# Scaling the long filter by its energy through four columns of short-convolution weights instead of through its spectrum

## What is computed

```python
def long_conv_bidir(u, h, bias):
    L = u.shape[1]
    k = jnp.concatenate([h[:, 0], jnp.zeros((1, HY_WIDTH), f32), h[:0:-1, 1]], axis=0)
    k = k * lax.rsqrt(jnp.sum(k * k, axis=0, keepdims=True))
    kf = jnp.fft.rfft(k, n=2 * L, axis=0)
    uf = jnp.fft.rfft(u.astype(f32), n=2 * L, axis=1)
    y = jnp.fft.irfft(uf * kf[None], n=2 * L, axis=1)[:, :L]
    return (y + u.astype(f32) * bias.astype(f32)).astype(u.dtype)

def short_conv(z, w, b):                      # 3 taps over the tokens
    ...
    return sum(zp[:, j:j + n] * w[j] for j in range(HY_SHORT)) + b

def hyena_branch(zb, sw, sb, filt, bias):
    zb = short_conv(zb, sw, sb)
    x0, x1, v = jnp.split(zb, 3, axis=-1)
    return x0 * long_conv_bidir(x1 * v, filt, bias)
```

## Time and profile before

| | |
|---|---|
| median of 3 runs | 2001.69 us (1999.43 to 2003.58) |
| the profiled execution: its own time | 2003.16 us |
| its span, first to last instruction | 2001.1 us |
| mean granted TensorE clock | 0.984 of full |
| busy: PE, PEld, DVE, ACT, POOL | 96%, 81%, 67%, 50%, 3% of the span |
| bytes read | 350.97 MB, 176 GB/s over the span |

### The profile page before, as it was taken

The page is one execution under the profiler, slowest core; times in us unless marked ns, Lnnn a source line. Parts: engine busy times, 40 slices in busy tenths (PEclk is TensorE's granted clock), DMA queues, the critical chain, the costliest instruction groups (busy, mean ns, idle before and its releaser), DMA issues.

```text
span 2001.1 us, 26355 instructions
## 1 busy us (share of the span) xinstructions
PE 1922.2 (96%) x10928; PEld 1621.3 (81%) x10928; DVE 1342.2 (67%) x1798; ACT 992.1 (50%) x1450; POOL 52.9 (3%) x49
## 2 busy tenths in 40 slices
PE   6999999999998899999899999999999999989998
PEld 3889888899887899988788886688888888768887
DVE  4878878878788777855655566665566555676555
ACT  2455544465544545554454455554445444565444
POOL 1400000000001000000000000000000000000000
PEclk7999999999999999999999999999999999999999
DMA  8534575434674443465355553355545555425553
GB/s 339 214 128 168 207 246 190 148 127 157 220 244 169 169 142 133 146 209 189 126 189 189 186 174 127 125 179 189 189 169 190 187 187 187 166 74 179 188 189 139
DMA packets 95686, 353.73 MB, mean 177 GB/s; under 512 B 10640, under 2 KB 10768, under 8 KB 94800
## 3 DMA queue, kind: packets, MB, share of 16 engines
q1 hardware_dynamic: 90864, 331.12, 47.8%
q0 software_dynamic: 4416, 19.43, 2.7%
q10 hardware_dynamic: 288, 1.51, 0.2%
HBM read 350.97 MB, written 1.05 MB: 176 GB/s over the span
## 4 chain that ended last, share of the span: by engine, by line
PE 85%; DVE 8%; ACT 4%; DMA 2%; issue 1%; SPq 0%; DVEq 0%; ACTq 0%
PE PS L606 25%; PE PS L608 25%; PE PS L607 25%; DVE w_lo L1934 3%; DMA raw<-weights 2%; ACT w_hi L1396 1%; PE PS L776 1%; PE PS L1047 1%; PE PS L795 1%; PE PS L1129 1%; PE PS L1010 1%; PE PS L880 1%; PE PS L861 1%; PE PS L738 0%; PE PS L756 0%
## 5 line engine op out<-in xcount | busy, mean ns | idle before, releaser
L1934 DVE TENSOR_TENSOR w_lo<-raw,w_hi 128x1024 fp32r<-128x1024 f32 x600 | 734.6, 1238 | 404.6 <-ACT w_hi L1396 403.5
L1396 ACT ACTIVATE w_hi<-raw 128x1024 fp32r<-128x1024 f32 x600 | 624.9, 1055 | 413.4 <-DMA raw<-weights 410.6
L606 PE MATMUL PS<-w_hi,h_hi 128*128 128x512 f32 (+1 forms) x1264 | 496.7, 393 | 18.7 <-DVE w_lo L1934 12.2
L608 PE MATMUL PS<-w_hi,h_lo 128*128 128x512 f32 (+1 forms) x1264 | 485.3, 384 | 0.0
L607 PE MATMUL PS<-w_lo,h_hi 128*128 128x512 f32 (+1 forms) x1264 | 484.9, 384 | 0.0
L606 PEld LDWEIGHTS PS<-w_hi,h_hi 128*128 128x128 f32 x1264 | 240.0, 190 | 71.7 <-DVE w_lo L1934 16.3
L608 PEld LDWEIGHTS PS<-w_hi,h_lo 128*128 128x128 f32 x1264 | 239.7, 190 | 47.5
L606 PE MATMUL PS<-h_hi,w_hi 128*128 128x256 f32 x928 | 271.5, 293 | 5.6 <-DVE h_lo L1952 5.1
L607 PEld LDWEIGHTS PS<-w_lo,h_hi 128*128 128x128 f32 x1264 | 240.5, 190 | 44.6 <-issue 1.4
L608 PE MATMUL PS<-h_hi,w_lo 128*128 128x256 f32 x928 | 263.7, 284 | 0.0
L607 PE MATMUL PS<-h_lo,w_hi 128*128 128x256 f32 x928 | 263.7, 284 | 0.0
(11 more groups left out here) (278 smaller groups left out, 1743.1 us busy)
## 6 DMA issues: line engine op xcount, KB each, us to landing
raw<-weights SPq DMA_DIRECT2D x614, 512.0 KB, 3.3
qk<-weights POOLq DMA_DIRECT2D x12, 512.0 KB, 4.4
v<-weights POOLq DMA_DIRECT2D x12, 512.0 KB, 4.3
x<-weights SPq DMA_DIRECT2D x6, 512.0 KB, 10.8
qk<-cond_in POOLq DMA_DIRECT2D x2, 1024.0 KB, 5.2
layer<-weights SPq DMA_DIRECT2D x3, 512.0 KB, 11.0
layer<-layer_in SPq DMA_DIRECT2D x1, 1536.0 KB, 6.7
layer<-layer_in POOLq DMA_DIRECT2D x1, 1536.0 KB, 8.3
```

The source lines that it names most:

```text
L606: pe.matmul(dst, hi, m_hi_, start=first, stop=False, **kw)
L608: return pe.matmul(dst, lo, m_hi_, start=False, stop=last, **kw)
L1396: nc.scalar.activation(w_hi[:, r, :], raw[:, r, :], ACT.Copy).then_inc(w_hi_ready, 1)
L1934: V.tensor_tensor(w_lo[:, r, :], raw[:, r, :], f32(w_hi[:, r, :]), ALU.subtract).then_inc(w_lo_ready, 1)
```

## The change

The spectrum is left undivided. Instead:

- TensorE turns the root's row into four columns: `filter_columns(l, bank)`, four products of a 128x128 piece of `conv_rt` with two columns of the constant 1/1024, into a PSUM bank. Layer 0's stand in pass 0's `keys_queries` behind the third pair of slots, layer 1's ahead of `keys_queries` of pass 2.
- VectorE takes the reciprocal of the four columns and multiplies the short convolution's weights and bias of x0's channels by them: `scale_short(l, bank)`, three instructions of at most 128x12.
- VectorE multiplies the bias row by the root and adds it to `spec`: `spectrum_bias(l)`, a 128x512 product and a 128x1024 sum, once in pass 0 and once in pass 2, ahead of the heads' reciprocal.
- Both reciprocals of 128x512 and GpSimd's four instructions go.

```diff
             energy_sums(1)
             spectrum_pairs(1)
-            spectrum_scale(0)
-            spectrum_bias(0)
...
             modulation_rows(1)
-            spectrum_scale(1)
             pool.wait_ge(src_ready, 16)
             pool.wait_ge(spec_ready, 1)
             pool.dma_start(layer[:, :], layer_in[1]).then_inc(layer_loaded[1], 16)
-            spectrum_bias(1)
...
                 if l == 1:
-                    pe.wait_ge(fil_rt, 1)
+                    pe.wait_ge(short_scaled, 1)
                 pe.matmul(PS[:, 2, :], ones[:, :], h_sq[l][:, 0, 0, :], start=True, stop=True).then_inc(fil_mm, 1)
+
+            def filter_columns(l, bank):
+
+                pe.wait_ge(fil_rt, l + 1)
+                for c in range(KB):
+                    mm = pe.matmul(PS[:, bank, 2 * c:2 * c + 2], conv_rt[:, l, c * P:(c + 1) * P], ones[:, 0:2], start=True, stop=True)
+                mm.then_inc(fil_columns, 1)
...
                     filter_taps(1)
+                if j == 2:
+                    filter_columns(0, 2)
...
             ctx_values(1, lambda: norm_total(5))
+            filter_columns(1, 3)
             keys_queries(2, 3)
...
             def taps(p, j):
+                if j == 0:
+                    act.wait_ge(short_scaled, l + 1)
...
-            def filter_scale(l):
-                dve.wait_ge(fil_rt, l + 1)
-                V.reciprocal(conv_rt[:, l, :], conv_rt[:, l, :]).then_inc(fil_rs, 1)
+            def scale_short(l, bank):
+
+                dve.wait_ge(fil_columns, l + 1)
+                link(V.reciprocal(conv_rs, PS[:, bank, 0:2 * KB].rearrange("p (c n) -> p c n", n=2)[:, :, 0]))
+                w = col(f"short_w{l}", 0, 36).rearrange("p (t f) -> p t f", t=3)[:, :, 0:KB]
+                b = col(f"short_b{l}", 0, KB)
+                link(V.scalar_tensor_tensor(w, w, P / D, conv_rs.rearrange("p (o f) -> p o f", o=1).to_broadcast([P, 3, KB]),
+                                            ALU.mult, ALU.mult))
+                V.scalar_tensor_tensor(b, b, P / D, conv_rs, ALU.mult, ALU.mult).then_inc(short_scaled, 1)
+
+            def spectrum_bias(l):
+
+                dve.wait_ge(spec_pair, l + 1)
+                dve.wait_ge(short_scaled, l + 1)
+                dve.wait_ge(layer_loaded[l], 16)
+                bias = conv_rt[:, l, :]
+                link(V.tensor_tensor(bias, bias, row("conv_row"), ALU.mult))
+                both = bias.rearrange("p (o c) -> p o c", o=1).to_broadcast([P, 2, BR])
+                V.tensor_tensor(spec[:, l, 0, :, :], spec[:, l, 0, :, :], both, ALU.add).then_inc(spec_ready, 1)
...
                 dve.wait_ge(tap_ready, 6 * p + j + 1)
+                dve.wait_ge(short_scaled, l + 1)
...
                 splits(c0 + part["gu"] + 2)
+                if p != 1:
+                    spectrum_bias(l)
...
-                    if (p, g) == (0, 0):
-                        filter_scale(1)
...
                 if j == 2:
                     filter_even_odd(1)
+                    scale_short(0, 2)
                 if j == 3:
                     ada_take(3, 3)
                     mod_part(0, ADA_TURNS, 2 * KD, 3 * KD)
                     mod_gates(0)
-                    filter_scale(0)
...
             split(c + 7 + AHEAD)
+            scale_short(1, 3)
             keys_queries(2)
```

More of the change, by code:

```diff
@@ L178, in build @@
         conv_rt = sb("conv_rt", [P, DEPTH, BR])
-        stat = sb("stat", [P, 88 + 14])
+        stat = sb("stat", [P, 88 + 14 + KB])
         arena = sb("arena", [P, 10752])
@@ L301, in build @@
         x_rt = stat[:, 62:64]
+        conv_rs = stat[:, 102:106]
         signal = stat[:, 82:84]
@@ L342, in build @@
         fil_evac = sem("fil_evac")
-        fil_rs = sem("fil_rs")
-        spec_scaled = sem("spec_scaled")
+        fil_columns = sem("fil_columns")
+        short_scaled = sem("short_scaled")
         spec_pair = sem("spec_pair")
@@ L554, in spectrum_pairs @@
                                         ALU.subtract).then_inc(spec_pair, 1)
-            def spectrum_scale(l):
-                pool.wait_ge(fil_rs, l + 1)
-                pool.wait_ge(spec_pair, l + 1)
-                rows = spec[:, l, :, :, :].rearrange("p a b c -> p (a b) c")
-                each = conv_rt[:, l, :].rearrange("p (o c) -> p o c", o=1).to_broadcast([P, 4, BR])
-                nc.gpsimd.tensor_tensor(rows, rows, each, ALU.mult).then_inc(spec_scaled, 1)
-            def spectrum_bias(l):
-                pool.wait_ge(layer_loaded[l], 16)
-                pool.wait_ge(spec_scaled, l + 1)
-                both = row("conv_row").rearrange("p (o c) -> p o c", o=1).to_broadcast([P, 2, BR])
-                nc.gpsimd.tensor_tensor(spec[:, l, 0, :, :], spec[:, l, 0, :, :], both, ALU.add).then_inc(spec_ready, 1)
             energy_sums(0)
```

## The result

The changed kernel takes 1982.73 us, median of five runs (1981.65 to 1983.32), against 1999.43 us for the kernel before, median of five (1997.82 to 2003.58). The ratio is 0.991 with a 95% interval of 0.990 to 0.9921, so it is faster by about 0.9%. The profiled execution took 1982.73 us with a span of 1980.8, 20.3 us less than the span of before.

A forecast was written before the change was run, and what follows sets the result against it. TensorE, busy 96%, was taken as the bound, so only its waits and slow clock count; 6.1 + 2.9 + 6.8 + 3.0 - 0.9 = 17.9 us off 2001.7 gave 1983.8, say 1984, with 8 in 10 for 1980 to 1991.

The forecast's parts named there:

- A: Layer 0, 97 to 104 us: without GpSimd's product and sum, TensorE's 4.37 us wait and its clock loss go, 6.1 us.
- B: 225 to 227 us: without the second reciprocal, `w_lo` ends 1.25 us earlier and the clock's loss goes, 2.9 us.
- C: 608 to 615 us: without GpSimd's layer 1 product, TensorE's 4.67 us wait and 2.10 of clock loss go, 6.8 us.
- D: 685 to 690 us: without GpSimd's layer 1 sum, TensorE's wait shrinks by 2.2 and the clock returns 0.8, 3.0 us.
- E: TensorE's two-column products: layer 0's four cost 0.9 us, layer 1's are hidden by a wait.
- F: VectorE's three small `scale_short` instructions: cost nothing, or 0.6 us if either layer's is late.
- G: `spectrum_bias` on VectorE, passes 0 and 2: 1.9 us each, hidden before a wait for ScalarE's heads root, cost 0.
- not what it says: Rival: something other than GpSimd, such as loads in flight, holds VectorE's long rows; 1999.7 us, chance 0.03.
- Waits shrink, but the clock isn't given back: Rival: TensorE's waits shorten but the lower clock behind them stays; 10 us gained, 1991.7, chance 0.17.
- The slower case: Rival: VectorE's bias sum delays TensorE's transform, 1.9 us in each of two passes; 2005 if stalls stay, chance 0.03.

## Why the prediction was right

The forecast was 1984, the median is 1982.73, and 1983.6 over all three series. The gain of 17.9 us stands against 16.7 by the medians, and 14.5 to 17.6 over the three series. That the time came out 1.1 us below the unrounded 1983.8 and not further off is in part luck: the median it started from, 2001.69 of three runs, is 1999.43 with two runs more, 2.3 us lower, and the gain was put 1.2 too high. Six of the seven terms came out within 0.3 us:

- **A, 6.1 forecast, 6.2 measured, and 6.8 when it is put back.** The end of VectorE's long row matched the end of GpSimd's, and that gave the cause and the size. The wait went whole, and the loss of clock with it. The 0.7 between the last two is the clock, which stayed low for 5.3 us behind the put-back wait and for 3.7 in the kernel before.
- **B, 2.9 forecast, 2.6 measured.** That the reciprocal's 3.35 us would not all come back was read from ScalarE's row. The wait that remains is 1.45 where 1.31 was forecast. It kept the clock, and the next edit at ScalarE's queue took it away.
- **C, 6.8 forecast, 6.6 measured, and 6.6 when it is put back.**
- **D, 3.0 forecast, 1.7 measured, 0.7 to 1.5 when it is put back.** This is the step that failed. Its wait did shrink, from 4.80 to 2.23, as the prediction worked out (1.7 to 2.3), and TensorE restarts 2.1 us earlier than before, for 2.2 forecast. But the 0.8 us for the clock had the wrong sign: "I let it fall, but for 3.10 us as at 384 instead of 4.68". The low stretch behind the shorter wait is 5.8 us long, 6.3 in the second profile, against 4.8 in the kernel before. That takes back (5.8 - 4.8) / 2 = 0.5 us, and 2.1 - 0.5 is, to 0.1, the 1.7 measured. The stretch of 384 us was taken for a property of short waits, and it was one case.
- **E, 0.9 forecast, 0.91 measured**, hidden in layer 1.
- **F and G, nothing**, with 1.1 and 1.65 us of the cover left where 1.2 was said.

Of the rivals, "not what it says" is refuted by the three kernels that put GpSimd's work back. "Waits shrink, but the clock isn't given back" is what happened at D alone. The slower case has its mechanism, shown with the longer bias sum, but needs about 1 us more on VectorE than the change puts there.

The prediction set its sum against the median and not against the profiled execution alone. From its own time it would have been 1985.3, 2.6 too high: 3.75 us of that execution were a late start that no profile of the changed kernel repeated.

Against the rule that the prediction took from the earlier trace rows, a wait under 2 us keeps 2.4 GHz and one over 2.2 loses it, the runs hold four cases. 2.15 us at the longer bias sum kept the clock. So did 2.21 us at 373 us in the second profile of the changed kernel, where the first has the same wait, 2.20, and lost it. Waits of 0.54, 0.96 and 0.95 in a row at D lost it. And 1.82 us at 316 us lost it for 3.4 us with the split ahead of the SiLU, the very wait that kept it at 1.81 in the kernel before (327 us). So as a rule it is refuted. At B, where it was used, the wait of 1.45 kept the clock in all three profiles of the changed kernel, and no run shows why it had to.

Nor is a lower clock always time lost. Behind the wait at 373 us it stayed low for 3.4 us in the first profile and not at all in the second, and the rows behind it come only 0.15 us earlier for that: with the clock up, TensorE waits for VectorE twice instead, 0.75 and 1.00 us, where it waited once, 0.62.

The changed kernel itself shows that the wait alone doesn't decide. In its third profile TensorE restarts at D behind the same 2.23 us, with the clock still up, waits a second time for 0.96, and runs slowly only then (the same 128x256 product takes 0.38 at the first restart and 0.58 at the second):

```profile
673.18 0.38 PE L590 MATMUL PS<-h_hi,w_hi 128*128 128x256 f32 x1 [2.23 <-DVE h_lo L1948]
...
675.56 0.58 PE L590 MATMUL PS<-h_hi,w_hi 128*128 128x256 f32 x1 [0.96 <-DVE h_lo L1948]
```

The Trainium skill (TensorE: Matmul & The Clock Gate, Part 1) says that the stretch over which the gate judges runs free of the kernel; the two profiles of one kernel agree with that.

What stays open: where the five longer of the fourteen executions lose their 3.5 us, of which no trace was kept, and what decides whether a wait of some 2 us costs the clock, and for how long.

## What to carry to other kernels

Look down the VectorE timeline for a tiny instruction with a length of microseconds, and compare its end with the end of a GpSimd instruction: a row of 3.83 us for two numbers a partition was worth 6 us here, although GpSimd was busy 3% of the time. Put a microsecond saved at a wait into the sum whole, and work out first which engine is late next. Put the clock behind the wait into it only where the wait goes whole; where 2 us of it stay, the lower clock can last longer than before, as it did at D. A quotient that is the same for a whole column belongs into a few columns ahead of the work and not into a row of 512 behind it.

## What the runs showed of the hardware

- Either of the two can be the one that is held. GpSimd's 128x1024 sum took 3.31 us behind a VectorE split that began 0.1 us before it, and 2.33 where VectorE was held. VectorE's 128x512 sum took 5.35 us under a GpSimd product whose row begins 0.2 us behind its own. So the starts in the trace don't tell which it will be.
- GpSimd's writing alone, 4 us of it, left VectorE's two-input instructions at 0.69 us.
- Behind 4.0 us of products with two moving columns TensorE's clock was 0.50 for 6 us, with no idle time ahead. The same number with 128 columns took 3.6 us and kept 1.00, and so did the 0.9 us of two columns that the change issues in layer 0.
- A wait of 2.15 us kept the clock once and one of 2.21 did, one of 1.82 lost it, and a wait of 2.23 lost it at once in one profile and 2.4 us later in another profile of the same kernel. The lower clock lasted 5.8 us behind a wait of 2.23 and 4.8 behind one of 4.80.
